# A split-precision decoder trunk on one core: where the first weight sum of a seven-product 2x2 block multiplication is made, and in which order its blocks are rounded

## The chip, the cores and the metric

One core of a Trainium2 chip runs the whole program. The metric is the device time of one execution in microseconds (us), the median over several runs; smaller is better.

## The reference, cut to what matters

Two layers, each FFN, mixer, FFN, on 256 tokens of width 1024. The four FFNs (F0, F1, F2, F3) are all alike:

```python
def swiglu(x, w_in, w_out):
    gate, up = jnp.split(x @ w_in, 2, axis=-1)      # w_in 1024 x 5632
    return (jax.nn.silu(gate) * up) @ w_out         # w_out 2816 x 1024
# x <- LN(ALPHA * x + 0.5 * swiglu(x, w_in, w_out))
```

The order of stages is F0, AB (attention and pooling), F1, F2, C (a gated recurrence), F3. The change touches the FFNs only.

## The kernel before, in words

**Split precision.** Every weight block lands in `raw` as float32. ScalarE (ACT) rounds it to a high part `w_hi` (`split_hi`, L503), VectorE (DVE) makes the rest `w_lo = raw - w_hi` (`split_lo`, L995), and TensorE (PE) adds three passes: high times high, high times rest, rest times high.

**Units.** A unit is 128 x 2048 numbers (1 MB), loaded as two transfers on SyncE's queue (SP) into one of three landing buffers. `raw_free` (L375) lets a load start when the last reader of that buffer is done. An FFN has eleven chunks of 256 hidden features. Each chunk needs two input units (called A and B here) and one output unit. Chunks 0 and 1 come in the plain form. Chunks 2 to 9 are feature-major: PE computes the hidden features transposed, in four up blocks (`up_block`, 16 matmuls each, L2012 and L2019), and ACT copies each block out of the one PSUM bank that they share (`up_copy`, L573), so up block b+1 waits for copy b. POOL folds the halves of the gate copies by accumulating transfers (`add_gates`, L1717), ACT takes the silu, DVE adds the halves of the up part and multiplies (`up_add`, `up_product`).

**Seven products.** For chunks 0 to 8 the output projection of a chunk, a 2x2 block product, is made of seven block products instead of eight (Winograd's form). Its weight unit, called P here, holds four plain blocks b12, b11, b22, b21, and four sums of them are needed. DVE makes the sums from `raw` into `SUM_PLACES` (`weight_sums`): t1 = b11-b12 and t3 = b22-b12 in one instruction (L1013), t2 = b22+t1 (L1017), t4 = b21-t2 (L1019). Three plain blocks are rounded into slot PLAIN (`split_plain_hi` L509, `split_plain_lo` L1001, 1536 columns), four sums into slot SUMS (`split_sums_hi` L515, `split_sums_lo` L1031, 2048 columns). Products 0, 1, 2 read PLAIN, products 3, 4, 5, 6 read SUMS.

**Order in chunk c.** Each engine runs a list written out by hand; nothing is reordered.
- PE (`feature_chunk`): up block 0; products 3 and 6 of P(c-2); up block 1; products 0, 1, 2 of P(c-1) begin; up block 2; their rest, which frees PLAIN (`plain_used`); product 4 begins; up block 3; products 4 and 5.
- ACT: the four copies, with the splits of A and B of chunk c+1 and of the sums between them, then the PLAIN split of P(c) before copy 3, then copy 3 and the gates' silu. In the last chunk (9), where there is no further P, the unit after B, called O here (the plain output unit of chunk 9), is split before copy 3; O takes slot PLAIN and so waits for `plain_used` too.
- DVE: add, product and hidden sums of chunk c-1 (`hidden_sums`); `weight_sums` of P(c-1); rests of the hidden sums; the rests of A, of the sums, of B and of P(c). Before chunk 2 it makes the rests of two units (chunk 2's A and B), hidden sums and the rest of P(1).
- POOL: `add_gates` for each chunk in turn.
- SP: P, A, B, P, A, B and so on, each when its buffer is free. P(c) uses the buffer of P(c-1), which is free when both the sums and the plain rest of P(c-1) are made.

After chunk 9 PE runs `project` for chunk 10, which waits for the last copy, and `down`, which waits for `last_hidT` (L1271) on DVE. The sums of the products leave PSUM by `kept` (L655), L664, `sums_out` and four accumulating transfers on POOL (`add_sums`, L1720).

Of the kernel before, what the change touches and what calls it, by code (L numbers as in the profile page):

```python
# [17 lines left out]
ALU = mybir.AluOpType  # L18
ACT = mybir.ActivationFunctionType
# [18 lines left out]
FIRST_FM = 2  # L38
N_FM = NC - 1 - FIRST_FM
# [36 lines left out]
def build(nc, x, positions, ln_gain, ln_bias, ffn1_w_in, ffn1_w_out, ffn2_w_in, ffn2_w_out, ab_w_in, ab_w_o,  # L76
          diff_lambda, diff_subln, pool_w, pool_scale, c_w_in, c_w_o, c_norm, hgrn_gamma, consts, out):
    with ExitStack() as ctx:
# [67 lines left out]
        w_step1, w_step2, w_sums = sem("w_step1"), sem("w_step2"), sem("w_sums")  # L146
        sums_hi, sums_lo, sums_used = sem("sums_hi"), sem("sums_lo"), sem("sums_used")
        sums_half = sem("sums_half")
# [119 lines left out]
        def region(a, *shape):  # L268
# [8 lines left out]
            return v  # L277

# [199 lines left out]
        def _(act):  # L478
# [26 lines left out]
            def split_plain_hi(n):  # L505

                landed(n)
                freed(plain_free[nth[n] - 1])
                nc.scalar.copy(w_hi[:, PLAIN, 0:1536], raw[:, n % RAW, 512:]).then_inc(plain_hi, 1)  # L509

            def split_sums_hi(name, n):

                act.wait_ge(w_sums, nth[n])
                freed(sums_free[nth[n] - 1])
                nc.scalar.copy(w_hi[:, SUMS], SUM_PLACES[name].rearrange("p a f -> p (a f)")).then_inc(sums_hi, 1)  # L515
# [65 lines left out]
            def ffn(name, m):  # L581
# [3 lines left out]
                if m == 0:  # L585
# [3 lines left out]
                    split_plain_hi(s0 + 4)  # L589
# [10 lines left out]
                else:  # L600
# [7 lines left out]
                    split_plain_hi(s0 + 4)  # L608
                    xT_split(m, 1)
                    act.wait_ge(hid_ready, hid + 1)  # L610
                    ffn_silu(name, 0, 1, G[1])
                    split_sums_hi(name, s0 + 4)
# [9 lines left out]
                split_plain_hi(s0 + 7)  # L622
                last = NC - 2
                for c in range(FIRST_FM, NC - 1):
                    n = s0 + 3 * c + 1
                    if c == FIRST_FM:
                        up_copy(name, c, 0)
                        hid_early_hi(name, c - 1)
                        hid_late_hi(name, c - 1)
# [3 lines left out]
                        up_copy(name, c, 2)  # L633
                        split_hi(n + 2)
                    elif c == FIRST_FM + 1:
                        up_copy(name, c, 0)
                        split_hi(n + 1)
                        hid_early_hi(name, c - 1)
                        hid_late_hi(name, c - 1)
                        up_copy(name, c, 1)  # L640
                        split_sums_hi(name, n)
                        split_hi(n + 2)
                        up_copy(name, c, 2)
                    else:
                        split_hi(n + 1)
                        up_copy(name, c, 0)
                        hid_early_hi(name, c - 1)
                        hid_late_hi(name, c - 1)
# [1866 lines left out]
```

## Time and profile before

| what | value |
|---|---|
| median of 3 runs | 966.76 us (966.62 to 968.57) |
| the profiled execution | 964.49 us, span 962.8 us |
| busy PE, PEld, DVE, ACT, POOL | 952.3, 806.8, 849.0, 620.4, 108.7 us |
| granted TensorE clock, mean | 0.998 |
| DMA, mean | 205 GB/s |

PE is TensorE's matmuls and PEld its weight loads, which run beside them. Busy time is time with at least one instruction on the engine. A line such as L573 is the line of the kernel that issued the instruction, and `[2.56 <-PE psum L2019]` behind a row of the timeline is how long the engine sat idle before it and what ended that.

### The profile page before, as it was taken

The numbers are of one execution on the slowest core, as the hardware profiler recorded it, in microseconds if no ns is written. First come the engines' busy times: TensorE is split into PE (matmuls) and PEld (weight loads), VectorE is DVE, ScalarE is ACT, GpSimd is POOL, SyncE is SP. The second block draws the span as 40 slices with busy tenths as digits, with TensorE's granted clock in tenths as the row PEclk, the third lists the DMA queues.
The fourth block names the chain that finished last, engine by engine and source line by source line (L and its number), as shares of the span: only waits on it lengthen the run. The fifth ranks groups of instructions, "written<-read, shape, count | busy, mean of one in ns | idle before, by whom it ended". The sixth has DMA issues, their size and how long they took to land.

```text
span 962.8 us, 13790 instructions
## 1 busy us (share of the span) xinstructions
PE 952.3 (99%) x4904; PEld 806.8 (84%) x4904; DVE 849.0 (88%) x1174; ACT 620.4 (64%) x727; POOL 108.7 (11%) x146
## 2 busy tenths in 40 slices
PE   9999999999999999999999999999999999999996
PEld 7888888888888888888888888888888888888885
DVE  5999998996898999889889989899898997999886
ACT  6776667436646667675576666549998546667660
POOL 0211111100210111110011101100100100111110
PEclk9999999999999999999999999999999999999999
DMA  9778877753656786876587777935243656786761
GB/s 306 240 228 234 280 235 223 232 178 129 223 180 205 217 244 193 236 227 206 173 237 235 239 231 232 271 124 184 89 131 115 235 192 190 215 242 194 237 162 55
DMA packets 140912, 197.31 MB, mean 205 GB/s; under 512 B 7280, under 2 KB 114336, under 8 KB 140720
## 3 DMA queue, kind: packets, MB, share of 16 engines
q1 hardware_dynamic: 126032, 173.56, 55.3%
q0 software_dynamic: 14256, 22.38, 11.1%
q8 instruction: 40, 0.66, 0.3%
q10 hardware_dynamic: 560, 0.52, 0.2%
q14 instruction: 24, 0.20, 0.1%
HBM read 182.79 MB, written 1.06 MB: 191 GB/s over the span
## 4 chain that ended last, share of the span: by engine, by line
PE 91%; DVE 5%; ACT 2%; issue 1%; DMA 1%; POOL 0%; DVEq 0%; SPq 0%; ACTq 0%
PE psum L2012 23%; PE psum L2026 15%; PE psum L2019 12%; PE psum L1821 12%; PE psum L1830 12%; PE psum L1825 12%; DVE w_lo L995 1%; PE psum L2402 1%; ACT w_hi L503 1%; PE psum L1814 1%; PE psum L2388 1%; DVE w_lo L1031 1%; DMA raw<-in_ffn_w_out 1%; DVE w_lo L1001 1%; PE psum L1996 1%
## 5 line engine op out<-in xcount | busy, mean ns | idle before, releaser
L995 DVE TENSOR_TENSOR w_lo<-raw,w_hi 128x2048 fp32r<-128x2048 f32 x125 | 285.1, 2284 | 20.9 <-ACT w_hi L503 20.8
L2012 PE MATMUL psum<-xT,w_hi 128*128 128x512 f32 x1024 | 254.2, 390 | 0.5
L503 ACT CAST w_hi<-raw 128x2048 fp32r<-128x2048 f32 x125 | 238.3, 1914 | 24.5 <-DMA raw<-in_ffn_w_in 15.0
L2012 PEld LDWEIGHTS psum<-xT,w_hi 128*128 128x128 f32 x1024 | 191.3, 188 | 44.8 <-ACT ffn_tok L573 3.2
L2019 PEld LDWEIGHTS psum<-xT,w_lo 128*128 128x128 f32 x1024 | 139.7, 190 | 10.0
L2019 PE MATMUL psum<-xT,w_lo 128*128 128x256 f32 x1024 | 142.8, 282 | 0.0
L1821 PE MATMUL psum<-w_hi,xT 128*128 128x512 f32 x447 | 128.7, 399 | 0.8 <-DVE arena L1538 0.4
L1830 PE MATMUL psum<-w_hi,xT 128*128 128x512 f32 x447 | 124.8, 390 | 0.2 <-DVE xT L1099 0.2
L1825 PE MATMUL psum<-w_lo,xT 128*128 128x512 f32 x447 | 124.7, 390 | 0.0
L1717 POOL DMA_DIRECT2D ffn_tok<-ffn_tok x64 | 55.0, 859 | 484.7 <-ACT ffn_tok L573 484.7
L1830 PEld LDWEIGHTS psum<-w_hi,xT 128*128 128x128 f32 x447 | 83.9, 188 | 18.3 <-DVE xT L1099 0.5
L1825 PEld LDWEIGHTS psum<-w_lo,xT 128*128 128x128 f32 x447 | 83.9, 188 | 17.7
L1821 PEld LDWEIGHTS psum<-w_hi,xT 128*128 128x128 f32 x447 | 80.8, 188 | 16.8 <-DVE ffn_tok L1160 0.8
L573 ACT COPY arena<-psum 128x512 f32<-128x512 f32 x64 | 37.6, 587 | 71.2 <-PE psum L2019 71.1
L1031 DVE TENSOR_TENSOR w_lo<-arena,w_hi 128x2048 fp32r<-128x2048 f32 x35 | 80.0, 2284 | 0.1
L1001 DVE TENSOR_TENSOR w_lo<-raw,w_hi 128x1536 fp32r<-128x1536 f32 x36 | 63.1, 1754 | 15.9 <-ACT w_hi L509 15.9
L573 ACT COPY ffn_tok<-psum 128x512 f32<-128x512 f32 x64 | 37.5, 586 | 59.3 <-PE psum L2019 45.1
L515 ACT CAST w_hi<-arena 128x2048 fp32r<-128x2048 f32 x36 | 68.9, 1915 | 10.5 <-DVE arena L1019 8.9
L2026 PE MATMUL psum<-w_hi,hT_hi 128*128 128x512 f32 x232 | 75.4, 395 | 0.0
L2026 PE MATMUL psum<-w_lo,hT_hi 128*128 128x512 f32 x232 | 75.1, 393 | 0.0
L2026 PE MATMUL psum<-w_hi,hT_lo 128*128 128x512 f32 x232 | 69.8, 393 | 0.0
L509 ACT CAST w_hi<-raw 128x1536 fp32r<-128x1536 f32 x36 | 53.5, 1485 | 14.5 <-PE psum L2026 7.9
(220 smaller groups left out, 1165.3 us busy)
## 6 DMA issues: line engine op xcount, KB each, us to landing
raw<-in_ffn_w_in SPq DMA_DIRECT2D x170, 512.0 KB, 5.2
raw<-in_ffn_w_out SPq DMA_DIRECT2D x88, 512.0 KB, 4.4
raw<-in_c_w_in SPq DMA_DIRECT2D x32, 512.0 KB, 4.7
ffn_tok<-ffn_tok POOLq DMA_DIRECT2D x64, 128.0 KB, 4.9
raw<-in_ab_w_in SPq DMA_DIRECT2D x16, 512.0 KB, 4.9
x_tok<-arena POOLq DMA_DIRECT2D x16, 256.0 KB, 7.3
raw<-in_ab_w_o SPq DMA_DIRECT2D x8, 512.0 KB, 4.2
raw<-in_c_w_o SPq DMA_DIRECT2D x8, 512.0 KB, 4.0
```

Of the source, the lines that this page charges most:

```text
L503: nc.scalar.copy(w_hi[:, slot_of[n]], raw[:, n % RAW]).then_inc(hi_ready, 1)
L515: nc.scalar.copy(w_hi[:, SUMS], SUM_PLACES[name].rearrange("p a f -> p (a f)")).then_inc(sums_hi, 1)
L573: nc.scalar.copy((UPS[name] if b // 2 else GATES)[:, b % 2], G[0]).then_inc(up_copied, 1)
L995: nc.vector.tensor_tensor(w_lo[:, slot_of[n]], raw[:, n % RAW], w_hi[:, slot_of[n]].bitcast(F32), ALU.subtract).then_inc(lo_ready, 1)
L1001: nc.vector.tensor_tensor(w_lo[:, PLAIN, 0:1536], raw[:, n % RAW, 512:], w_hi[:, PLAIN, 0:1536].bitcast(F32), ALU.subtract).then_inc(plain ...
L1031: nc.vector.tensor_tensor(w_lo[:, SUMS], SUM_PLACES[name].rearrange("p a f -> p (a f)"), w_hi[:, SUMS].bitcast(F32), ALU.subtract).then_in ...
L1821: nc.tensor.matmul(dst, a_hi, b_hi, start=first, stop=False)
L1825: ins = nc.tensor.matmul(dst, a_hi, b_lo, start=False, stop=final and last)
L1830: ins = nc.tensor.matmul(dst, a_lo, b_hi, start=False, stop=final and last)
L2012: nc.tensor.matmul(G[0], w_hi[:, slot_of[n + kh], at:at + P], xT_both[:, 4 * kh + k].rearrange("p a s -> p (a s)"), start=kh == k == 0, st ...
L2019: ins = nc.tensor.matmul(G[0][:, 0:SEQ], w_lo[:, slot_of[n + kh], at:at + P], xT_hi[:, 4 * kh + k], start=False, stop=kh == 1 and k == 3)
L2026: return nc.tensor.matmul(PROD[p], a[:, A_OF[p] * P:(A_OF[p] + 1) * P], w[:, slot, part * 512:(part + 1) * 512], start=start, stop=stop)
```

## The change

The unit P is loaded in the same way, but its first sum is made in place, in the landing buffer: the first quarter of `raw` becomes s1 = b12+b11. For P(0) and P(1) DVE does it (`first_sum`, 128 x 512), for P(2) to P(8) POOL does it with two accumulating transfers of 128 x 256 each, issued behind the gate transfers of the same chunk. The whole unit is now rounded into PLAIN (2048 columns), and only three sums go into SUMS (1536 columns): n2 = b22-s1 and, in one instruction, n2+b11 and n2+b21. Some signs turn, and with them those of the sums taken out at the end of an FFN. Product 4 becomes a plain product. So PE sets `plain_used` only behind up block 3, and POOL, ACT and DVE wait for each other in a new order: ACT's PLAIN split of P(c) stands behind the silu and waits for the first sum, DVE's PLAIN rest stands in the next chunk, in front of the rests of A, of the sums and of B, and ACT splits A between copy 1 and copy 2 in all chunks.

```diff
+HERE = 2
+        def first_sum_ready(name, n):
+            f, c = SILUS[name], (n - phases[name] - 4) // 3
+            if c < HERE:
+                return first_sum_here, HERE * f + c + 1
+            return first_sum_added, 32 * ((N_PROD - HERE) * f + c - HERE + 1)
...
 ACT
-            def split_plain_hi(n):
+            def split_plain_hi(name, n):
                 landed(n)
+                act.wait_ge(*first_sum_ready(name, n))
                 freed(plain_free[nth[n] - 1])
-                nc.scalar.copy(w_hi[:, PLAIN, 0:1536], raw[:, n % RAW, 512:]).then_inc(plain_hi, 1)
+                nc.scalar.copy(w_hi[:, PLAIN], raw[:, n % RAW]).then_inc(plain_hi, 1)
...
                 for c in range(FIRST_FM, NC - 1):
+                    up_copy(name, c, 0)
+                    hid_early_hi(name, c - 1)
+                    hid_late_hi(name, c - 1)
                     if c == FIRST_FM:
                         up_copy(name, c, 1)
                         split_hi(n + 1)
                         split_sums_hi(name, n)
...
                     else:
                         split_sums_hi(name, n)
                         up_copy(name, c, 1)
+                        split_hi(n + 1)
+                    up_copy(name, c, 2)
+                    split_hi(n + 2)
                     if c == last:
-                        act.wait_ge(plain_used, N_PROD * (f + 1))
-                        nc.scalar.activation(kept[0], PROD[0], ACT.Copy, scale=NORMS[name][1]).then_inc(copied_out, 1)
                         split_hi(n + 3)
-                    else:
-                        split_plain_hi(n + 3)
                     up_copy(name, c, 3)
                     gates_silu(name, c)
+                    if c < last:
+                        split_plain_hi(name, n + 3)
+                act.wait_ge(plain_used, N_PROD * (f + 1))
+                nc.scalar.activation(kept[0], PROD[0], ACT.Copy, scale=NORMS[name][1]).then_inc(copied_out, 1)
...
 DVE
+            def first_sum(n):
+                w = raw[:, n % RAW]
+                dve.wait_ge(raw_landed[n % RAW], 32 * (n // RAW))
+                nc.vector.tensor_tensor(w[:, 0:512], w[:, 0:512], w[:, 512:D], ALU.add).then_inc(first_sum_here, 1)
...
                 split_lo(s0 + 6)
+                first_sum(s0 + 7)
                 hidden_sums(name, 1)
                 split_plain_lo(s0 + 7)
...
-                    weight_sums(name, n, 0)
-                    weight_sums(name, n, 1)
...
+                    weight_sums(name, n)
...
+                    else:
+                        split_plain_lo(n)
+                        hid_early_lo(name, c - 1)
+                        hid_late_lo(name, c - 1)
+                        beside(name, c)
+                        split_sums_lo(name, n)
+                        split_lo(n + 1)
                     split_lo(n + 2)
-                    if c < last:
-                        split_plain_lo(n + 3)
...
 POOL
+            def first_sum(name, c):
+                n = phases[name] + 4 + 3 * c
+                w = raw[:, n % RAW]
+                pool.wait_ge(raw_landed[n % RAW], 32 * (n // RAW))
+                for cs in (slice(0, 256), slice(256, 512)):
+                    pool.dma_start(w[:, cs], w[:, 512 + cs.start:512 + cs.stop], accum_op=ALU.add
+                                   ).then_inc(first_sum_added, 16)
...
+                    if HERE <= c < N_PROD:
+                        first_sum(name, c)
...
 PE, feature_chunk
-                token_rest(last, 0, 1, 2).then_inc(plain_used, 1)
-                pe.wait_ge(sums_hi, nth[p])
+                token_rest(last, 0, 1, 2)
                 high(4)
                 up_block(name, n, c, 3)
+                weight_rest(4)
+                token_rest(last, 4).then_inc(plain_used, 1)
+                pe.wait_ge(sums_hi, nth[p])
                 high(5)
                 pe.wait_ge(sums_lo, nth[p])
-                weight_rest(4, 5)
-                token_rest(last, 4, 5).then_inc(pairs_done if last else early_used, 1)
+                weight_rest(5)
+                token_rest(last, 5).then_inc(pairs_done if last else early_used, 1)
```

At the start of an FFN the first sum of P(0) is made by DVE ahead of `weight_sums`, ACT rounds P(0) behind one more silu (in F1, F2 and F3), and product 4 joins product 0. At its end the one addition to x of 128 x 1024 (L1237) becomes an addition and a subtraction of 128 x 512.

## Rows read from the trace of the kernel before

**Rows 1.** The page, part 1: busy time of each engine.
```profile
PE 952.3 (99%) x4904; PEld 806.8 (84%) x4904; DVE 849.0 (88%) x1174; ACT 620.4 (64%) x727; POOL 108.7 (11%) x146
```

**Rows 2.** Who waited for whom: engine, line, waited for, us, times, longest.
```profile
PEld psum L2012 <- ACT ffn_tok L573: 3.2, 7, 0.6
```

**Rows 3.** The chain in order of time, F1: start, us, what.
```profile
350.18 1.81 PE psum L2012 x8
...
366.11 1.81 PE psum L2012 x8
```

**Rows 4.** Groups of instructions: busy us, mean ns, idle before.
```profile
L1031 DVE TENSOR_TENSOR w_lo<-arena,w_hi 128x2048 fp32r<-128x2048 f32 x35 | 80.0, 2284 | 0.1
...
L515 ACT CAST w_hi<-arena 128x2048 fp32r<-128x2048 f32 x36 | 68.9, 1915 | 10.5 <-DVE arena L1019 8.9
...
L1001 DVE TENSOR_TENSOR w_lo<-raw,w_hi 128x1536 fp32r<-128x1536 f32 x36 | 63.1, 1754 | 15.9 <-ACT w_hi L509 15.9
...
L1013 DVE TENSOR_TENSOR arena<-raw 128x1024 f32<-128x1024 f32 x36 | 43.8, 1218 | 3.1 <-DMA raw<-in_ffn_w_out 2.8 <-issue 0.2
...
L1017 DVE TENSOR_TENSOR arena<-raw,arena 128x512 f32<-128x512 f32 x36 | 24.9, 691 | 1.2
```

**Rows 5.** Timeline of F1 up to chunk 2's second up block.
```profile
288.70 1.22 DVE L1419 CAST decay<-arena 128x2048 fp32r<-128x2048 f32 x1
...
294.68 4.48 DVE L995 TENSOR_TENSOR w_lo<-raw,w_hi 128x2048 fp32r<-128x2048 f32 x2
...
296.48 1.49 ACT L509 CAST w_hi<-raw 128x1536 fp32r<-128x1536 f32 x1
...
300.53 0.59 ACT L573 COPY ffn_tok<-psum 128x512 f32<-128x512 f32 x1 [2.56 <-PE psum L2019]
...
301.49 0.64 PEld L2012 LDWEIGHTS psum<-xT,w_hi 128*128 128x128 f32 x3
```

**Rows 6.** Timeline of one undisturbed chunk of F1.
```profile
350.88 0.90 SPq L422 DMA_DIRECT2D raw<-in_ffn_w_out  x2
...
353.79 6.22 SPq L393 DMA_DIRECT2D raw<-in_ffn_w_in  x4
353.86 0.86 POOL L1717 DMA_DIRECT2D ffn_tok<-ffn_tok  x1 [3.31 <-ACT ffn_tok L573]
...
361.45 0.69 DVE L1067 TENSOR_TENSOR arena<-arena 128x512 f32<-128x512 f32 x1 [0.29 <-ACT arena L573]
```

**Rows 7.** DMA issues, 349.5 to 350.5 us: KB each, median us to landing.
```profile
ffn_tok<-ffn_tok POOLq DMA_DIRECT2D x1, 128.0 KB, 2.7
```

**Rows 8.** DMA issues, 350.8 to 352 us.
```profile
raw<-in_ffn_w_out SPq DMA_DIRECT2D x2, 512.0 KB, 4.3
```

**Rows 9.** DMA issues, 353.5 to 355 us.
```profile
ffn_tok<-ffn_tok POOLq DMA_DIRECT2D x1, 128.0 KB, 5.1
```

**Rows 10.** DMA issues of the whole program.
```profile
x_tok<-arena POOLq DMA_DIRECT2D x16, 256.0 KB, 7.3
```

**Rows 11.** Timeline of the end of F1.
```profile
421.57 0.60 ACT L655 ACTIVATE arena<-psum 128x512 f32<-128x512 f32 x1 [0.34 <-PE psum L2026]
...
423.99 2.29 DVE L995 TENSOR_TENSOR w_lo<-raw,w_hi 128x2048 fp32r<-128x2048 f32 x1 [1.63 <-ACT w_hi L503]
...
424.56 0.59 ACT L573 COPY arena<-psum 128x512 f32<-128x512 f32 x1 [0.60 <-PE psum L2019]
424.60 0.62 PE L2026 MATMUL psum<-w_lo,hT_hi 128*128 128x512 f32 x2
...
426.89 1.07 PE L1821 MATMUL psum<-w_hi,xT 128*128 128x512 f32 x4
...
437.30 0.42 DVE L1271 TENSOR_TENSOR hT_lo<-psum,hT_hi 128x256 fp32r<-128x256 f32 x1 [0.60 <-ACT hT_hi L676]
...
438.95 0.62 PE L1830 MATMUL psum<-w_hi,hT_lo 128*128 128x512 f32 x2
...
444.17 0.42 DVE L1160 TENSOR_TENSOR ffn_tok<-psum,ffn_tok 128x256 f32<-128x256 f32 x1 [0.21 <-ACT ffn_tok L540]
```

More of the change, by code:

```diff
@@ L514, in split_sums_hi @@
                 freed(sums_free[nth[n] - 1])
-                nc.scalar.copy(w_hi[:, SUMS], SUM_PLACES[name].rearrange("p a f -> p (a f)")).then_inc(sums_hi, 1)
+                nc.scalar.copy(w_hi[:, SUMS, 0:1536], SUM_PLACES[name][:, 1:].rearrange("p a f -> p (a f)")
+                               ).then_inc(sums_hi, 1)
             def split_hi_piece(n, k):
@@ new lines, in split_plain_lo, with weight_sums @@
+                nc.vector.tensor_tensor(w_lo[:, PLAIN], raw[:, n % RAW], w_hi[:, PLAIN].bitcast(F32), ALU.subtract
+                                        ).then_inc(plain_lo, 1)
+            def first_sum(n):
+                w = raw[:, n % RAW]
+                dve.wait_ge(raw_landed[n % RAW], 32 * (n // RAW))
+                nc.vector.tensor_tensor(w[:, 0:512], w[:, 0:512], w[:, 512:D], ALU.add).then_inc(first_sum_here, 1)
+            def weight_sums(name, n):
+                w = raw[:, n % RAW].rearrange("p (a f) -> p a f", a=4)
+                s1, b22, n2 = w[:, 0], w[:, 2], SUM_PLACES[name][:, 1]
+                dve.wait_ge(*first_sum_ready(name, n))
+                if nth[n] > 1:
+                    dve.wait_ge(sums_lo, nth[n] - 1)
+                nc.vector.tensor_tensor(n2, b22, s1, ALU.subtract).then_inc(w_step, 1)
+                dve.wait_ge(w_step, nth[n])
+                nc.vector.tensor_tensor(SUM_PLACES[name][:, 2:4], w[:, 1:4:2], n2.unsqueeze(1).to_broadcast([P, 2, 512]),
+                                        ALU.add).then_inc(w_sums, 1)
@@ L1031, in split_sums_lo @@
-                nc.vector.tensor_tensor(w_lo[:, SUMS], SUM_PLACES[name].rearrange("p a f -> p (a f)"),
-                                        w_hi[:, SUMS].bitcast(F32), ALU.subtract).then_inc(sums_lo, 1)
+                sums = SUM_PLACES[name][:, 1:].rearrange("p a f -> p (a f)")
+                parts = ((0, 512, sums_first), (512, 1536, sums_lo)) if halves else ((0, 1536, sums_lo),)
+                for c0, c1, signal in parts:
+                    nc.vector.tensor_tensor(w_lo[:, SUMS, c0:c1], sums[:, c0:c1], w_hi[:, SUMS, c0:c1].bitcast(F32),
+                                            ALU.subtract).then_inc(signal, 1)
@@ L1963, in _ @@
             A_OF = (2, 3, 6, 0, 4, 5, 1)
-            B_OF = ((PLAIN, 0), (PLAIN, 2), (PLAIN, 1), (SUMS, 3), (SUMS, 0), (SUMS, 1), (SUMS, 2))
+            B_OF = ((PLAIN, 1), (PLAIN, 3), (PLAIN, 2), (SUMS, 2), (PLAIN, 0), (SUMS, 0), (SUMS, 1))
             ALONE = (0, 4, 5, 6)
@@ L1981, in products @@
                 if half:
[L1982 removed]
+                    pe.wait_ge(sums_first, 1)
                 else:
```

89 lines of the change are left out of this document (22 added, 67 removed).

## The prediction, on record before the changed kernel ran

> **What bounds the kernel now.** I read the page's busy times first. TensorE is busy 952.3 of a span of 962.8 us, VectorE 849.0 [rows 1]: PE is the bound nearly everywhere, and its matmuls number the same before and after this change. So a lighter DVE can give back only what PE now waits. The list of waits gives that directly. The one wait of PE inside the feature-major chunks that repeats is that of an up block for ACT's copy of the one before it: 3.2 us in 7 places [rows 2]. It comes up in the first chunks of each FFN, where DVE's queue is the late one. In an undisturbed chunk the chain in order of time repeats its second up block from 350.18 to 366.11, that is every 15.93 us, with PE on the chain throughout [rows 3]. The ceiling of the gain is therefore 3.2 us, and every new wait is measured against it.
>
> **The change part by part.**
>
> *DVE's work.* Today a P unit costs DVE 1.22 + 0.69 + 0.69 for the sums, 1.75 for the plain rest, 2.28 for the sums' rest [rows 4], the third instruction taken as long as the second, of the same shape. After it, 0.69 + 1.22 for the sums, 2.28 plain and 1.75 sums, and 0.69 more for P(0) and P(1) only. That is 0.69 less for 28 of 36 units, 19 us of DVE in all. PE hides all of it but the 3.2 us. I take the whole **-3.2 us**: in chunks 2 and 3 DVE loses both 0.69 and the plain rest of 1.75 from in front of `up_add`.
>
> *ACT's work.* The two casts swap sizes and their sum stays.
>
> *Start of the chunks, P(1).* Today ACT rounds P(1) at 296.48, long before it has to copy up block 0 at 300.53; it sat idle 2.56 us before that copy [rows 5]. After the change this cast waits for the first sum, which DVE makes only behind two rests that run from 294.68 for 4.48 us, to 299.16 [rows 5]. First sum to 299.88, cast of 1.92 [rows 4] to 301.8, copy of 0.59 to 302.3. PE's second up block loads its first weights at 301.49 today [rows 5], without a wait, and would start at 302.35: **+0.85 us**, in each of four FFNs, 3.4. Who waits behind the cast on ACT: copy 0, the hidden parts, copy 1. In F1 there is more. DVE used the time before 288.70 for a sums' rest, then made the table cast of 1.22 us [rows 5]; now it must wait for a hidden product first and makes the sums' rest behind it, so that the table cast pushes the hidden sums out by 1.4 us; PE then waits some 0.75 us more by my count. F0 has the plain split behind the landing and the first sum, 0.3 us more net. Together **+4.45 us**; bounds 2.4 (only half of 0.85 is paid, plus extras of half size) and 6.
>
> *Waits for the first sum in the loop.* Count from the undisturbed chunk. `up_add` started at 361.45, so one chunk earlier at 345.5 [rows 3, 6]. In the new order B's rest ends just before it, and I take 345.8. Add, product and hidden sums take 2.5 us with their semaphores, the new sums 0.69 + 1.22, the plain rest 2.28 [rows 4]: 352.5, when the landing buffer of P is free. SP issues the next P at 352.7 where it now does at 350.88 [rows 6], its second transfer 0.45 later, landing after 4.3 [rows 8]: 357.45. POOL wakes and issues the first accumulating transfer, and the second behind it, which I put at 0.95 together (an estimate; one issue alone is busy 0.86 [rows 6]): the second starts at 358.4. What does a transfer of 128 KB by POOL take? The gate transfer alone on the queues took 2.7 us [rows 7], the one issued at 353.86 beside the loads of A issued at 353.79 [rows 6] took 5.1 [rows 9]. In the new order A's buffer is free behind the early and late rests (1.24), the sums' rest 1.75 and A's own rest 2.28, at 357.7, so A is loaded just when the first sum is made. I take 5.1, since the row has the same company: the first sum is there at 363.5. ACT needs 1.92 + 0.59 from there to have up block 0 copied: 366.05, and PE starts the second up block at 366.11 [rows 3]. So it just fits, or is a few tenths late, since there are two such transfers. A wait is paid at every second chunk: one paid at a chunk moves PE, but not the chain behind the next P, by its length. That makes 14 payments in four FFNs. Taken: 0.2 us each, **+2.6 us**. Bounds: 0, and (with the 7.3 us of the accumulating transfers into x [rows 10]) 2.2 x 14 = 31 us.
>
> The row shows a gate transfer nearly doubled by company [rows 7, 9]. The Trainium skill, page "DMA: Bandwidth & Descriptors", section "Queues, rings and completion order", says that an engine takes turns between queue rows only at packet boundaries; the trace agrees, with 2.7 against 5.1 us. The same page, section "Anatomy of one DMA — SWDGE (gpsimd) path", fits one such transfer by 2.0 us plus its bytes over 436 KB per us, an estimate of 2.3 us here; by it there would be no wait at all and the sum would be 2.6 us less.
>
> *End of an FFN.* Here I expect the largest term. In chunk 9 ACT splits O, into slot PLAIN, ahead of copy 3. PLAIN was freed before up block 3, at 421.5 (L655 at 421.57 waited for it) [rows 11]. Now it is freed behind up block 3 and two matmuls, as the row at 424.60 shows, near 425.0. The cast runs 425.0 to 426.9, copy 3 to 427.45 instead of 425.15. PE's `project`, at 426.89 today [rows 11], waits for copy 3: **+0.6 us**. DVE is worse off: O's rest moves from 423.99 [rows 11] to 426.95, and `up_add` stands behind it, so the whole DVE list, with the hidden part, the sums out and three more rests, is 3.0 us late. By my count over the timeline it has 0.9 us of idle time on its way to `last_hidT`, 0.60 of it right in front [rows 11]. I count it through to 440.0 instead of 437.30, ending 440.4, while PE reaches the first pass that reads it at 438.95 + 0.6 [rows 11]: 0.85 more. The hidden product of the second tile, at 444.17 [rows 11], comes behind a norm on DVE and costs 0.75 more. Sum 2.2 us per FFN with a following stage, and 0.6 in F3, where DVE has no units of a next stage to split: **+7.2 us**. Bounds: 0.6 x 4 = 2.4, and 3.0 x 4 = 12. The addition to x in two parts costs 0.16 us more of DVE and lies inside this.
>
> *The rest.* POOL issues 56 more transfers; it is busy 108.7 us [rows 1], so nobody queues there. kept[0] is copied later, and PE needs it only a projection later.
>
> **Sum.** 4.45 + 2.6 + 7.2 - 3.2 = +11.05 us on the profiled execution's 964.49: 975.5. The median of the runs lies 2.3 above that execution, so I forecast **977.8 us**.
>
> **The rivals.**
> 1. *The first sum lands as if alone* (2.7 us [rows 7]): no waits in the loop, 964.49 + 8.45 + 2.3 = 975.2. For it: A is issued only as the sum starts. Against: so it was for the gates. The fit of the Trainium skill's page "DMA: Bandwidth & Descriptors" is the rule that points here.
> 2. *The end is absorbed*: DVE's lateness of 3.0 us is made up in the last projection, and only 0.6 x 4 remains, with no loop waits: +3.65, 970.4. For it: many waits on DVE there are for ACT. Against: DVE idles only 0.9 us before `last_hidT`.
> 3. *The first sum takes longer*: 6.2 us, halfway from 5.1 to 7.3 [rows 9, 10], two accumulating transfers and two loads at once. Then 1.1 us x 14 = 15.4 instead of 2.6, and 990.6 us. For it: three queued accumulating transfers take 7.3. Against: those have twice the bytes.
> 4. *Costs and gain cancel*: the two start and end costs are each paid at their lower bound and the gain is whole: 2.4 + 2.4 - 3.2 = +1.6, 968.4 or a little less.
> 5. *DVE's relief decides*: ACT's two late casts (P(1) and O) are covered by waits that PE has anyway, and 3.2 us of PE's waits go: 963.6. It would decide if copy 0 of chunk 2 still ended by 301.5 and copy 3 of chunk 9 by 426.9. Against: the orders of ACT and DVE are fixed, and both dates follow from rows alone.
> 6. *It doesn't do what it says*: if the accumulating transfers gave no relief because DVE still waits at `up_add` for copy 3 (0.29 us idle there today [rows 6]), DVE's 19 us turn into idle time. That holds in the undisturbed chunks in any case, and is in the sum.
>
> **How the numbers follow.** A measurement here tells apart about 0.2%, 1.9 us. Chances: forecast 0.40, rival 1 0.13, rival 2 0.15, rival 3 0.16, rival 4 0.08, rival 5 0.08. Slower is then 0.84, within 0.2% 0.08, faster 0.08. The range reaches from a little below rival 2 to just short of rival 3's time, 968.5 to 990.0. The forecast's own range is 973 to 983.
>
> **What would show it.** In the profile of the changed kernel: ACT's plain cast of P(1) begins near DVE's first sum, and the second up block of chunk 2 waits 0.8 us for copy 0. Undisturbed chunks still take 15.9 us, and DVE is busy 0.7 us less in each. The list of waits has ACT's plain cast waiting for the accumulating transfer in many chunks. At FFN ends ACT's split of O waits for PE some 1.5 us and more, `project` waits for copy 3, and a `down` pass for L1271. I am wrong if the waits of PE for ACT in the chunks fall below 3.2 us in total, or if an FFN from its chunk 2 to its last `down` is not 3 us or more longer than before.

## The result, and the profile after

The changed kernel takes **1024.47 us** (median of 5 runs, 1017.31 to 1026.87) against 966.76 (965.39 to 970.18) on the same chip: ratio 1.057, 95% interval 1.054 to 1.060. It is 57.7 us slower, where 11 were forecast. Its profiled run has a span of 1023.7 us, 60.9 more than before.

The page of the changed kernel, busy times and the software queue:
```profile
PE 970.7 (95%) x4904; PEld 813.2 (79%) x4904; DVE 833.8 (81%) x1150; ACT 612.4 (60%) x727; POOL 157.5 (15%) x202
...
q0 software_dynamic: 22320, 29.72, 15.7%
```
DVE is 15.2 us lighter than in [rows 1], near the forecast 19, and it bought nothing. PE is busy 18 us *more* with the same 4904 matmuls: some of them ran at a lower clock.

The changed kernel's groups (busy us, mean ns, idle before) that answer to [rows 4]:
```profile
L998 DVE TENSOR_TENSOR w_lo<-raw,w_hi 128x2048 fp32r<-128x2048 f32 x36 | 82.4, 2290 | 6.9 <-ACT w_hi L519 6.3
...
L525 ACT CAST w_hi<-arena 128x1536 fp32r<-128x1536 f32 x36 | 53.3, 1481 | 0.0
...
L1016 DVE TENSOR_TENSOR arena<-raw,arena 128x1024 f32<-128x1024 f32 x36 | 44.1, 1225 | 1.2
```
The compute prices were right. The waits of the changed kernel (engine, line, waited for, us, times, longest), against [rows 2]:
```profile
POOL raw L1716 <- DMA raw<-in_ffn_w_out: 84.4, 28, 4.8
ACT w_hi L519 <- issue: 68.5, 23, 4.5
...
PEld psum L2020 <- ACT ffn_tok L584: 42.4, 25, 3.3
...
DVE arena L1014 <- DMA raw<-raw: 19.8, 18, 2.2
...
PEld psum L1829 <- ACT hT_hi L673: 8.3, 2, 4.3
...
PEld psum L1829 <- ACT arena L584: 3.6, 4, 0.9
```
Read from PE backwards. L2020 is the up block: its waits for copy 0 were 3.2 us in 7 places and are 42.4 in 25. Copy 0 stands behind ACT's plain cast L519, and that cast waits 68.5 us for something the profile shows only as "issue"; DVE's L1014, which waits for the same first sum, names it: the transfer raw<-raw. It lands late in nearly every chunk:
```profile
raw<-raw POOLq DMA_DIRECT2D x56, 128.0 KB, 5.5
```
From each FFN's first up block of chunk 2 to its last of chunk 9, the four FFNs take 136.10, 133.70, 135.82 and 135.42 us instead of 124.24, 124.04, 124.45 and 124.32: **44.0 of the 60.9 us** are there, the waits at the chunks' start among them. The other 16.9 lie from there to the next FFN: 6.5 (F0 to F1), 7.4 (F1 to F2), 2.0 (F2 to F3), 0.9 (after F3) and 0.1 ahead of F0.

In F1, PEld's waits at the second up blocks of chunks 2 to 9 are 0.88, 3.26, none, 1.73, 0.20, 1.63, none, 1.78: the start, and then every second chunk, as forecast, but some eight times its size each. The other three FFNs don't keep to that: F2 has 2.42, 1.65 and 2.05 in chunks 3, 4 and 5, F3 waits in every chunk from 5 to 9, F0 in 3, 5, 6, 8 and 9. In all, 21 of the 28 chunks behind a sum by POOL wait, 38.9 us together. The largest wait has a tail. Timeline of the changed kernel, chunk 3 of F1:
```profile
337.41 1.90 ACT L519 CAST w_hi<-raw 128x2048 fp32r<-128x2048 f32 x1 [4.55 <-issue]
...
339.22 0.58 ACT L584 COPY ffn_tok<-psum 128x512 f32<-128x512 f32 x1
...
339.85 3.06 PEld L2020 LDWEIGHTS psum<-xT,w_hi 128*128 128x128 f32 x8 [3.26 <-ACT ffn_tok L584]
339.85 3.57 PE L2020 MATMUL psum<-xT,w_hi 128*128 128x512 f32 x8 [2.83 <-ACT ffn_tok L584]
...
345.36 1.98 PE L2020 MATMUL psum<-xT,w_hi 128*128 128x512 f32 x8
```
and the windows of the same stretch (us, engines, granted clock, DMA share, GB/s):
```profile
339.84:343.40 3.56, 3.55 (x10) 2.86 (x11) 3.56 (x4) 2.26 (x3) 0.85 (x1) 0.55 0.41 77
343.40:347.00 3.60, 3.60 (x22) 3.11 (x21) 1.14 (x2) 2.40 (x2) 0.85 (x1) 1.00 0.82 266
374.77:378.30 3.53, 3.53 (x19) 3.09 (x20) 3.53 (x4) 2.69 (x4) 0.86 (x1) 1.00 0.38 62
```
After PE had stood still for 2.83 us the eight matmuls took 3.57 us instead of 1.98, at a granted clock of 0.55, mostly the lower level of 1.2 GHz, and the next up block came 5.51 us later instead of 3.93: 1.6 us on top of the wait. After the wait of 1.3 us (PE) at 374.77 the clock stayed at 1.00. The same loss of 1.6 to 1.7 us follows five of the 21 waits (PE idle for 1.8 to 2.8 us), 8.3 us in all. The length of the wait alone doesn't decide it: after 1.99 us at 535.59 the clock stayed at 1.00. The Trainium skill, page "TensorE: Matmul & The Clock Gate", section "What's actually happening", has a gate that passes half or all of the pulses by how busy PE was of late; the trace agrees, with 0.55 against 1.00.

### The profile page after: what moved, and what is told of

It reads as the page before. It is cut to its first block, busy times and chain, and to the rows that moved or that the text cites. A ratio compares the mean times of both kernels' runs of the same rounds, so it can differ in the third digit from the quotient of the medians.

```text
span 1023.7 us, 13823 instructions
## 1 busy us (share of the span) xinstructions
PE 970.7 (95%) x4904; PEld 813.2 (79%) x4904; DVE 833.8 (81%) x1150; ACT 612.4 (60%) x727; POOL 157.5 (15%) x202
## 4 chain that ended last, share of the span: by engine, by line
PE 62%; DVE 12%; DMA 10%; issue 8%; ACT 6%; SPq 1%; POOL 1%; DVEq 0%; ACTq 0%
PE psum L2020 16%; PE psum L2034 9%; PE psum L1829 8%; PE psum L1833 8%; PE psum L1838 8%; PE psum L2027 8%; DMA raw<-in_ffn_w_out 4%; DVE w_lo L992 4%; DMA raw<-in_ffn_w_in 2%; DMA raw<-raw 2%; ACT w_hi L512 2%; DVE w_lo L998 2%; ACT w_hi L519 1%; ACT ffn_tok L584 1%; DMA raw<-in_ab_w_in 1%
## 5 line engine op out<-in xcount | busy, mean ns | idle before, releaser
L992 DVE TENSOR_TENSOR w_lo<-raw,w_hi 128x2048 fp32r<-128x2048 f32 x125 | 285.6, 2288 | 90.4 <-ACT w_hi L512 90.2
L2020 PE MATMUL psum<-xT,w_hi 128*128 128x512 f32 x1024 | 262.8, 400 | 32.0 <-ACT ffn_tok L584 31.8
L512 ACT CAST w_hi<-raw 128x2048 fp32r<-128x2048 f32 x125 | 238.5, 1916 | 39.0 <-DMA raw<-in_ffn_w_in 11.1
L2020 PEld LDWEIGHTS psum<-xT,w_hi 128*128 128x128 f32 x1024 | 194.4, 192 | 83.4 <-ACT ffn_tok L584 42.4
L2027 PEld LDWEIGHTS psum<-xT,w_lo 128*128 128x128 f32 x1024 | 141.1, 192 | 10.5
L519 ACT CAST w_hi<-raw 128x2048 fp32r<-128x2048 f32 x36 | 68.7, 1907 | 83.1 <-issue 68.5
L998 DVE TENSOR_TENSOR w_lo<-raw,w_hi 128x2048 fp32r<-128x2048 f32 x36 | 82.4, 2290 | 6.9 <-ACT w_hi L519 6.3
L2034 PE MATMUL psum<-w_lo,hT_hi 128*128 128x512 f32 x232 | 80.4, 394 | 0.0
L2034 PE MATMUL psum<-w_hi,hT_lo 128*128 128x512 f32 x232 | 75.1, 393 | 0.0
L1025 DVE TENSOR_TENSOR w_lo<-arena,w_hi 128x1536 fp32r<-128x1536 f32 (+2 forms) x37 | 63.1, 1708 | 0.1
L1716 POOL DMA_DIRECT2D raw<-raw x56 | 48.7, 1023 | 84.4 <-DMA raw<-in_ffn_w_out 84.4
```

The source lines that it names most:

```text
L512: nc.scalar.copy(w_hi[:, slot_of[n]], raw[:, n % RAW]).then_inc(hi_ready, 1)
L519: nc.scalar.copy(w_hi[:, PLAIN], raw[:, n % RAW]).then_inc(plain_hi, 1)
L992: nc.vector.tensor_tensor(w_lo[:, slot_of[n]], raw[:, n % RAW], w_hi[:, slot_of[n]].bitcast(F32), ALU.subtract).then_inc(lo_ready, 1)
L998: nc.vector.tensor_tensor(w_lo[:, PLAIN], raw[:, n % RAW], w_hi[:, PLAIN].bitcast(F32), ALU.subtract).then_inc(plain_lo, 1)
L1025: nc.vector.tensor_tensor(w_lo[:, SUMS, c0:c1], sums[:, c0:c1], w_hi[:, SUMS, c0:c1].bitcast(F32), ALU.subtract).then_inc(signal, 1)
L2020: nc.tensor.matmul(G[0], w_hi[:, slot_of[n + kh], at:at + P], xT_both[:, 4 * kh + k].rearrange("p a s -> p (a s)"), start=kh == k == 0, st ...
```

## The experiments

Each is an edit of the changed kernel. The first question was whether the late landing is the cause, and of how much; the rivals were the new order of the rests on DVE, the order at an FFN's end, and the clock. The kernel before took 966 to 967 us (median) on each occasion. "Product 4 early" and the like name edits of chunk 9, the last feature-major one.

**First sums by DVE.** `first_sum` of P(2) to P(8) goes to DVE, ahead of B's rest.
```diff
-HERE = 2
+HERE = 9
                         split_lo(n + 1)
+                    if c < last and c < HERE:
+                        first_sum(n + 3)
                     split_lo(n + 2)
```


> The changed kernel, but DVE makes all first sums (one add of 128x512 in front of B's rest, where DVE stood idle 1.6 us waiting for ACT); orders of ACT and PE as changed. Theory T (the landing of the transferred first sum, late on the cycle load - sum - casts - load, makes the chunks of an FFN 9.7 to 11.9 us longer each, 44 us in four): the 32 chunks return to 15.9 to 16.2 us and the time falls by 40 to 46 us, to 979 to 985. Rival O (the new order of the rests on DVE and the later release of PLAIN make the chunks long, whoever makes the sum): over 1010 us, chunks stay over 16.8 us.


Measured: **977.47 us** (976.33 to 978.79), ratio 1.012 (1.010 to 1.014). 47.0 us are gone, a little more than the 40 to 46 expected. The chunks are back at 15.93 us but for one or two in each FFN (to 16.8). Waits of this kernel:
```profile
PEld psum L1831 <- ACT arena L584: 3.6, 4, 0.9
...
PEld psum L2022 <- ACT ffn_tok L584: 3.4, 4, 0.9
...
PEld psum L1831 <- ACT hT_hi L673: 2.9, 3, 2.3
```
So moving the first sums from POOL to DVE gives 47 us back, and the order of the rests on DVE, which is the changed one here too, is not the cause. Not all of it is the loop: of the 49.1 us between the two profiled spans (1023.7 and 974.6), 42.3 lie between an FFN's first up block of chunk 2 and its last of chunk 9, and 6.8 between the FFNs. What stays is 0.9 us at each start, 0.9 at each `project`, and a wait for the hidden part.

**The end, first try.** O split behind copy 3 and the silu, its rest behind `up_product`.
```diff
-                    if c == last:
-                        split_hi(n + 3)
                     up_copy(name, c, 3)
                     gates_silu(name, c)
                     if c < last:
                         split_plain_hi(name, n + 3)
+                    else:
+                        split_hi(n + 3)
...
-                split_lo(n + 3)
                 up_add(name, last)
                 up_product(name, last)
+                split_lo(n + 3)
```


> The changed kernel, but in the last chunk ACT splits O only behind copy 3 and the silu, and DVE makes O's rest behind up_product. Theory E (O's split, waiting for PLAIN, holds copy 3, up_add and with them the whole end of an FFN, and the units loaded next): PE's waits of 4.3 and 3.6 us for the hidden part's copy at two FFN ends go, 9 to 14 us less than the changed kernel, 1011 to 1016. Rival (the end is late because O's rest is late in any order, as PLAIN is freed late): less than 4 us gained, since O's rest comes 2 us later still here.


Measured: 1025.92 us (1024.0 to 1033.68), ratio 1.061. No gain. In its profile (of the slowest execution) PE's waits for copy 3, 3.6 us in the changed kernel, are gone, but those for the hT_hi copy (ACT's rounding of the last chunk's hidden part, L673, which `down` reads) are 12.3 us in 3 places instead of 8.3 in 2: O's rest comes later still, and the load behind it too. This run does not separate the two. That DVE's queue, my reason for the end term, is not what PE waits for is seen in the changed kernel: there no matmul waits for L1268 (`last_hidT`, L1271 before), and PEld waits for L1154 (L1160 before) 1.3 us in 2 places.

**One transfer instead of two.**
```diff
-            return first_sum_added, 32 * ((N_PROD - HERE) * f + c - HERE + 1)
+            return first_sum_added, 16 * ((N_PROD - HERE) * f + c - HERE + 1)
...
-                for cs in (slice(0, 256), slice(256, 512)):
-                    pool.dma_start(w[:, cs], w[:, 512 + cs.start:512 + cs.stop], accum_op=ALU.add
-                                   ).then_inc(first_sum_added, 16)
+                pool.dma_start(w[:, 0:512], w[:, 512:D], accum_op=ALU.add).then_inc(first_sum_added, 16)
```


> The changed kernel with one accumulating transfer of 128x512 instead of two of 128x256. Theory T with issue as a part of the lateness: the second issue started 0.87 us behind the first, so the sum is there 0.3 to 0.9 us sooner, and at 14 to 28 payments the time falls by 5 to 20 us. Rival B (the bytes beside the loads set the landing, not the number of issues): within 4 us of the changed kernel.


Measured: 1007.89 us (1002.18 to 1013.27), ratio 1.044 (1.038 to 1.049), 16.6 us less. One transfer of 256 KB takes 6.0 us, hardly more than one of 128 KB (5.5), and the second issue, 0.87 us on POOL, is saved:
```profile
raw<-raw POOLq DMA_DIRECT2D x28, 256.0 KB, 6.0
```

**Loads kept apart.** SP holds A's loads until the first sum is there.
```diff
-                    with sp.Fori(0, NPAIR) as i:
...
+                    for c in range(2 * NPAIR):
+                        a = s0 + 5 + 3 * c
+                        if c >= HERE:
+                            sp.wait_ge(first_sum_added, 32 * ((N_PROD - HERE) * SILUS[name] + c - HERE + 1))
+                        for kh in range(2):
+                            load_gate_up(a + kh, None, wi, kh, c + 2)
+                        load_rows(a + 2, None, wo, c + 1)
```


> The changed kernel, but SP issues A's loads only once the first sum of the P before it has landed, so the two do not run side by side (the loads of chunks 2 to 9 are written out instead of looped). Theory C (company: a transfer of POOL takes 2.7 us alone and 5.5 beside loads): the first sum lands in about 3.5 us, 2 us sooner, most waits go, 20 to 40 us less, 985 to 1005. Rival (its length is its own, or A's later landing at once takes its place as the wait): less than 8 us gained, or a loss.


Measured: 1021.29 us (1018.63 to 1026.2), ratio 1.059, far from the 985 to 1005 that theory C expected. The DMA issues of this kernel:
```profile
raw<-in_ffn_w_out SPq DMA_DIRECT2D x88, 512.0 KB, 6.0
...
ffn_tok<-ffn_tok POOLq DMA_DIRECT2D x64, 128.0 KB, 6.5
...
raw<-raw POOLq DMA_DIRECT2D x56, 128.0 KB, 3.1
```
Without the company of the loads the transfer takes 3.1 us instead of 5.5. The company isn't gone but moved: the gate transfers take 6.5 (3.6 in the changed kernel), the loads of output units, P's among them, 6.0 (4.4), and POOL's wait for P's landing is 155.0 us instead of 84.4. So this run shows that company lengthens the transfer, and not what a shorter one would be worth.

**Every second sum by POOL.** My theory by then was that lateness is carried from P to P, since load, sum and rests take as long as a chunk.
```diff
-HERE = 2
+HERE = (0, 1, 3, 5, 7)
...
-                    if HERE <= c < N_PROD:
+                    if c < N_PROD and c not in HERE:
                         first_sum(name, c)
...
+                    if c in HERE:
+                        first_sum(n + 3)
```


> DVE makes the first sum of P(3), P(5), P(7), POOL that of P(2), P(4), P(6), P(8), as in the changed kernel. All POOL sums replaced by DVE sums took 47.0 us off (1024.5 to 977.5), over 28 chunks, 1.68 us each. Theory L (lateness is carried from one P to the next, since the round trip of load, sum and plain rest is as long as a chunk): a chunk of DVE between two of POOL gives the next P its early issue back, so a POOL chunk then pays only what a single one is short of, some 0.7 us (first sum there at 352.7 + 5.1 + 0.9 + 5.5 = 364.2 against 363.5), 16 of them: 977.5 + 11 = 989, chunks behind a DVE sum at 15.9 to 16.1 us. Rival N (each POOL sum pays by itself, nothing is carried): 16 x 1.68 = 27, 1004.


Measured: **1017.06 us** (1012.23 to 1024.79), ratio 1.053 (1.049 to 1.057). Both expectations fail: 16 sums by POOL cost 39.6 us over the 977.47, 2.5 each, nearly as much as all 28 together. So nothing needs to be carried: all 16 wait, and none of the chunks between them. Each sum that meets an undisturbed PE pays in full; one behind a paid wait meets a PE that is late already and pays less. That is the prediction's "every second chunk", but it is only partly so: in the changed kernel the sums behind a paid wait pay nothing in F1 (or 0.2 us) and in part elsewhere. By PEld's waits for copy 0 without the four starts, 16 sums cost 34.9 us here and 28 cost 38.9 there. Timeline of this kernel, one clean cycle, P(8) of F1:
```profile
424.12 1.98 PE L2024 MATMUL psum<-xT,w_hi 128*128 128x512 f32 x8
...
426.59 0.90 SPq L433 DMA_DIRECT2D raw<-in_ffn_w_out  x2
...
431.84 5.00 SPq L404 DMA_DIRECT2D raw<-in_ffn_w_in  x4
...
432.23 1.74 POOL L1720 DMA_DIRECT2D raw<-raw  x2 [3.40 <-DMA raw<-in_ffn_w_out]
...
439.25 0.69 DVE L1016 TENSOR_TENSOR arena<-raw 128x512 f32<-128x512 f32 x1 [1.03 <-DMA raw<-raw]
439.30 1.90 ACT L521 CAST w_hi<-raw 128x2048 fp32r<-128x2048 f32 x1 [3.24 <-issue]
...
441.10 0.58 ACT L586 COPY ffn_tok<-psum 128x512 f32<-128x512 f32 x1
...
441.73 1.66 PE L2024 MATMUL psum<-xT,w_hi 128*128 128x512 f32 x6 [1.52 <-ACT ffn_tok L586]
```
Undisturbed, the up block at 441.73 would have started at 424.12 + 15.93 = 440.05. This is the cycle that the prediction forecast, ending at the kernel before's
```profile
365.95 1.98 PE L2012 MATMUL psum<-xT,w_hi 128*128 128x512 f32 x8
```
The prediction compared with 366.11, where the chain of [rows 3] has this block, while its other dates come from the timeline, which has it at 365.95. The two cycles side by side, in us before the block's undisturbed start in the timeline:

| | forecast | measured |
|---|---|---|
| P's load issued | 13.25 | 13.46 |
| P landed, first accumulating issue | 8.50 | 7.82 |
| second one starts | 7.55 | 6.95 |
| first sum is there | 2.45 | 0.80 |
| up block can start | -0.10 | -1.68 |

Against the forecast "just fits", 0.60 us are lost by the landing and the issue, 1.05 by the transfer (6.15 instead of 5.1), and 0.16 by the two dates of one block. P(2) is dearer: in the changed kernel's F1 its load is issued 1.4 us later against PE (324.63, where the up block began at 320.79), so its wait is 3.3 us (2.4 to 3.1 in the other FFNs), and there the low clock follows; it does so in three of the four FFNs.

**The start.** With DVE's sums, the first sum of P(1) ahead of the rest of B, in F1 to F3.
```diff
+                if m:
+                    first_sum(s0 + 7)
                 split_lo(s0 + 6)
-                first_sum(s0 + 7)
+                if m == 0:
+                    first_sum(s0 + 7)
```


> All first sums on DVE in the loop (977.5 us), and in F1, F2 and F3 the first sum of P(1) stands in front of the rest of chunk 2's B instead of behind it. Theory S (copy 0 of chunk 2 is late because ACT's cast of P(1) waits for that sum): the waits of the up block for copy 0, 0.9 us in each FFN, go in three FFNs: 974.8, between 974.5 and 975.5. Rival (the hidden sums, 0.7 us later on DVE for the same reason, or the cast itself is late by PE): 977.5, no change.


Measured: 977.13 us (974.04 to 980.44). No change in the median. The waits at the start went as expected (3.4 us in 4 places became 0.9 in one), but those for the hT_hi copy at FFN ends grew from 2.9 to 6.9 us.

**Product 4 early.** With DVE's sums; in chunk 9 alone PE ends product 4 before up block 3.
```diff
                 high(4)
-                up_block(name, n, c, 3)
+                if c < NC - 2:
+                    up_block(name, n, c, 3)
                 weight_rest(4)
                 token_rest(last, 4).then_inc(plain_used, 1)
+                if c == NC - 2:
+                    up_block(name, n, c, 3)
```


> All first sums on DVE in the loop (977.5 us), and in the last feature-major chunk alone PE does the rests of product 4 in front of up block 3, so that slot PLAIN is free there as early as in the kernel before. Theory E (the end of an FFN costs since O is split late, and with O's rest everything behind it on DVE and the loads of the next stage): the waits for copy 3 (3.6 us in 4 places) and for the first hT_hi copy of the next stage (2.9 us in 3) go: 971.0, between 969 and 973. Rival (as when O's split was put behind copy 3, the lateness comes from elsewhere, from the loads): 977.5, at best 976.


Measured: 982.01 us (981.21 to 983.35), ratio 1.017 (1.015 to 1.018), 4.5 us *more*, where theory E expected 971 and its rival no change. The waits for copy 3 are gone as expected, but those for the hT_hi copy are 10.9 us instead of 2.9. (That copy is of the last chunk of the same FFN, not of the next stage, as the expectation has it.)

**These two together.**


> The first sums on DVE in the loop, the first sum of P(1) early in F1, F2 and F3, and product 4 in front of up block 3 in the last feature-major chunk. If the two terms add: 977.5 - 2.7 - 6.5 = 968.3, within 0.2% of the kernel before (966.4). If DVE's relief of 0.69 us per chunk is not there any more (DVE makes the first sum again) and the second DVE wait stays, 970 to 972. The rival (neither does anything): 977.5.


Measured: 979.71 us (977.91 to 984.75). That is neither the sum of the two (968.3) nor a gain at all. The terms don't add while something else at the end can eat them.

What eats them is seen in the changed kernel's timeline at the end of F1:
```profile
448.76 0.59 ACT L584 COPY arena<-psum 128x512 f32<-128x512 f32 x1 [1.53 <-PE psum L2027]
...
449.24 1.91 ACT L512 CAST w_hi<-raw 128x2048 fp32r<-128x2048 f32 x1
...
449.72 1.98 PE L2020 MATMUL psum<-xT,w_hi 128*128 128x512 f32 x8
...
453.50 13.98 SPq L402 DMA_DIRECT2D raw<-in_ffn_w_in  x8
...
455.15 2.29 DVE L992 TENSOR_TENSOR w_lo<-raw,w_hi 128x2048 fp32r<-128x2048 f32 x1 [1.67 <-ACT w_hi L512]
...
457.40 2.62 POOL L1728 DMA_DIRECT2D x_tok<-arena  x3 [10.83 <-ACT arena L661]
...
468.73 1.90 ACT L512 CAST w_hi<-raw 128x2048 fp32r<-128x2048 f32 x1 [5.30 <-DMA raw<-in_ffn_w_in]
...
470.53 0.37 ACT L673 CAST hT_hi<-psum 128x256 fp32r<-128x256 f32 x1
470.95 0.50 PEld L1829 LDWEIGHTS psum<-w_hi,hT_hi 128*128 128x128 f32 x2 [4.29 <-ACT hT_hi L673]
```
O's buffer is given back by O's rest at 457.44 us; the load into it, for the next FFN, is issued at 457.47 and 457.88, beside three accumulating transfers into x from 457.40 on. The second half lands 10.8 us after its issue. ACT splits that unit at 468.73, in front of the hT_hi copy, and PE waits 4.29 us for the copy. In the kernel before, the same load was issued at 426.31 and 426.72, O's rest having begun at 423.99 [rows 11], with the transfers into x from 426.62 on; its second half took 6.4 us, and nobody waited. The PE wait at 470.95 is followed by the low clock too (0.50 from there to 476.20). O is late not only through `plain_used`: in the changed order ACT splits B *behind* copy 2 (the cast at 449.24), and O behind B.

**A and B early in chunk 9.** With DVE's sums, in that chunk alone.
```diff
 ACT
-                    else:
+                    elif c < last:
...
+                    else:
+                        split_hi(n + 1)
+                        split_sums_hi(name, n)
+                        up_copy(name, c, 1)
+                        split_hi(n + 2)
                     up_copy(name, c, 2)
-                    split_hi(n + 2)
+                    if c < last:
+                        split_hi(n + 2)
...
 DVE
+                    elif c == last:
+                        split_plain_lo(n)
+                        hid_early_lo(name, c - 1)
+                        split_lo(n + 1)
+                        hid_late_lo(name, c - 1)
+                        beside(name, c)
+                        split_sums_lo(name, n)
```


> First sums on DVE in the loop (977.5 us). In the last feature-major chunk alone ACT splits A in front of the sums and B in front of copy 2, and DVE makes A's rest in front of the sums' rest, as the kernel before does. Theory Q (in the changed order B's rest is late, so the loads that take its buffer and O's buffer, for the next stage, are issued 2.5 us later against PE and the second of them runs beside the three transfers into x and takes 12 us instead of 6.8; ACT, which splits that unit in front of the hidden part, then holds PE): that load is issued some 1.5 us earlier than without it, the waits for the hT_hi copy shrink or go, 973 to 976 us. Rival W (O's split behind up block 3 holds that load in any case, since O's buffer is the one): no change, 977.5. The copy 3 waits (3.6 us) stay under both.


Measured: 978.78 us (976.32 to 979.6). No gain: rival W holds, O is still split behind up block 3.

**The same, with product 4 early.**


> As the run before, and product 4 in front of up block 3 in that chunk, so that O is split early too. Alone that second edit made it worse (982.0 us). Theory Q: now both buffers are given back about 1 us after where the kernel before does, before the transfers into x start; the waits for the hT_hi copy (10.9 us) and for copy 3 (3.6 us) go, and 969 to 972 us result. Rival X (product 4 in front does harm by itself, since the transfers into x start earlier by it): 977 or more, and the load is again beside those transfers.


Measured: **970.65 us** (968.83 to 971.92), ratio 1.004 (1.003 to 1.006). Each edit alone gave +1.3 and +4.5; together they take 6.8 off. Timeline of this kernel, end of F1:
```profile
424.57 1.91 ACT L512 CAST w_hi<-raw 128x2048 fp32r<-128x2048 f32 x1 [1.08 <-PE psum L2049]
...
426.51 2.29 DVE L998 TENSOR_TENSOR w_lo<-raw,w_hi 128x2048 fp32r<-128x2048 f32 x1 [1.66 <-ACT w_hi L512]
...
429.67 2.62 POOL L1743 DMA_DIRECT2D x_tok<-arena  x3 [8.78 <-ACT arena L667]
...
435.07 1.90 ACT L512 CAST w_hi<-raw 128x2048 fp32r<-128x2048 f32 x1
...
439.09 0.37 ACT L679 CAST hT_hi<-psum 128x256 fp32r<-128x256 f32 x1 [2.12 <-PE psum L2019]
```
O's rest ends at 428.80, the load is issued at 428.83, 0.84 us ahead of the transfers into x, and lands in 5.0 us (median of its halves); ACT's third cast waits for nothing, and the hT_hi copy waits for PE, not PE for it.

**All three edits.**


> As the run before, and the first sum of P(1) early in F1, F2 and F3. If the start (2.0 us of PE waits seen gone in the chunks) and the end add: 967 to 970 us; what then is left against the kernel before is F0's start and 0.6 us of DVE's first sums in chunk 3. Rival: 975 or more, if the start's gain is eaten at the FFN ends, as it was when it stood alone (977.1).


Measured: **966.64 us** (965.61 to 968.67, 12 runs), ratio 1.000 (0.999 to 1.001). The start's edit, worth nothing alone, is now worth 4.0 (2.6 between the two profiled spans).

What the edits at the end share is seen in the second half of the load that takes O's buffer, by the ends of F0, F1 and F2 (us; waits below 0.3 left out):

| kernel | issued, against the first transfer into x | issue to landing | PEld's wait for the hT_hi copy |
|---|---|---|---|
| before | 0.1 behind | 6.8, 6.4, 6.0 | none |
| changed | 0.5 behind | 10.5, 10.8, 6.6 | 4.0, 4.3, none |
| DVE's sums | 0.5 behind | 8.8, 6.9, 6.7 | 2.3, 0.4, none |
| DVE's sums, start | 0.5 behind | 9.9, 10.0, 6.6 | 3.4, 3.5, none |
| DVE's sums, product 4 | 0.6 behind | 10.8, 11.8, 10.8 | 3.3, 4.3, 3.3 |
| DVE's sums, start, product 4 | 0.6 behind | 11.7, 10.8, 10.6 | 4.2, 3.3, 3.1 |
| DVE's sums, A and B | 0.5 behind | 8.7, 6.7, 6.5 | 2.2, none, none |
| DVE's sums, A and B, product 4 | 0.4 ahead | 8.2, 5.5, 5.8 | none |
| DVE's sums, all three | 0.4 ahead | 6.0, 7.9, 5.1 | none |

Where the landing takes 8.7 us or more, PE waits 2.2 us or more; where it takes 8.2 or less, 0.4 at most.

**The three edits under POOL's sums.**


> The changed kernel, with its sums on POOL, and the three other edits (B and A of the last feature-major chunk early, product 4 in front of up block 3 there, the first sum of P(1) early in F1 to F3). With the sums on DVE the same three edits took 10.9 us off (977.5 to 966.6). If the late landing in the loop is a term of its own, it stands alone here: 966.6 + 47.0 = 1013.6, between 1010 and 1018, every late chunk start as in the changed kernel, and nothing at the FFN ends. Rival (the terms hide one another, since a PE that is late in the last chunk gives the loads time): 1005 or less, or 1021 and more if the edits do nothing under POOL's sums.


Measured: 1011.39 us (1008.64 to 1013.78), ratio 1.047 (1.045 to 1.049). The landing in the loop stands alone with 1011.39 - 966.64 = 44.8 us, next to the 47.0 of the first experiment. Between the two profiled spans it is 42.6 us, all of it from an FFN's first up block of chunk 2 to its last of chunk 9. This run also bounds the clock: it fell in only two places of the loops, and the loops are still this long. Its longest wait in F1 was followed by no fall:
```profile
334.36 2.11 PE L2036 MATMUL psum<-xT,w_hi 128*128 128x512 f32 x8 [2.70 <-ACT ffn_tok L584]
...
334.36:337.90 3.54, 3.54 (x19) 3.11 (x20) 3.54 (x4) 2.70 (x4) 0.85 (x1) 1.00 0.46 57
```

## Why the prediction was wrong

By the chain of runs, the 57.8 us over the last kernel are **47.0** for the sums back on DVE (1024.47 to 977.47), **6.8** for the order in chunk 9 (to 970.65) and **4.0** for the start (to 966.64). The forecast had 2.6 for the loop, 7.2 for the end and 4.45 for the start, less 3.2. The first step is not all loop: by itself the loop is 44.8 us in medians and 42.6 in spans. The changed kernel's own executions lie from 1017.31 to 1026.87, so the first step is known, by my estimate, to some 3 us.

- **Waits for the first sum in the loop: the step that failed.** Its mechanism and its place were right: copy 0 waits behind the PLAIN cast, which waits for the first sum, and P's load was issued within 0.2 us of the forecast. The term was mis-sized: +2.6 us, where the runs show 42.6 to 44.8. I found a first sum that "just fits, or is a few tenths late" and took 0.2 us; a clean cycle is 1.7 late. "So it just fits" was a difference of two dates 13 us apart, each of its transfers priced by a single row: 4.3 for P's landing (POOL woke 5.64 after the first issue, not 4.75) and 5.1 for the accumulating transfer (6.15; the model was one gate transfer, here are two in a row), and the date to keep was read 0.16 us late. Then up blocks wait for it in 21 places, not 14 (the list's 25 less the four starts): "every second chunk" holds in F1 alone. P(2)'s wait is 2.4 to 3.3 us, since DVE is later in chunk 2, and the fall of the clock adds 1.6 to 1.7 us in five places. The upper bound, 2.2 x 14 = 31 us, was itself too low, and I left it out of the range.
- **Rival 3** (a transfer of 6.2 us) had the duration that was measured, and still forecast 15.4 us, since it kept the early landing and the 14 places and had no clock. **Rival 1** (2.7 us, and the 2.3 us estimated by the fit in the Trainium skill's page "DMA: Bandwidth & Descriptors", section "Anatomy of one DMA — SWDGE (gpsimd) path") is refuted beside loads: 5.5 us in the median. Kept apart it took 3.1, so the company is what lengthens it, though how the DMA engines share their time no trace here shows; the fit is near a transfer with little company, and the measurement decides here.
- **The start of the chunks: right in mechanism and place, near in size.** Copy 0 held the second up block by 0.84 to 0.93 us (0.85 forecast) in each FFN, and mending it in three FFNs gave 4.0 us in medians, 2.6 in profiled spans, where the waits mended add up to some 2.6. F1's table cast was not tested by itself.
- **The end: near in size by luck, mostly wrong in reason.** 6.8 us against 7.2, but the changed kernel has 16.9 us more between its FFNs. With DVE's sums 10.1 are left of it, and the edits in chunk 9 take 11.2 there and cost 3.4 in the loops; 6.8 (7.8 in spans) is what remains. `project` waited 0.9 us for copy 3 in each FFN (0.6 forecast). The rest was not DVE's lateness on its way to `last_hidT`, for which no matmul of the changed kernel waited, but the second half of a load for the next stage, issued 0.5 us behind the transfers into x, where the kernel before has 0.1, and landing late, with the low clock behind the wait. The forecast had not seen that B moves behind copy 2 either. Rival 2, in which the end is absorbed, is refuted.
- **DVE's relief, -3.2 us:** not seen. Where the loop was mended, DVE makes the first sum itself, so that kernel has no relief and can't show it; under POOL's sums, 44.8 us of lateness cover it.

**What stays open:** why that load took 10.5 and 10.8 us at two ends of the changed kernel and 6.6 at the third, and 6.7 to 8.8 in the kernel with DVE's sums, at the same distance of issues (0.5 us). That the order of these transfers is behind the results of the start and of product 4 alone is read from their traces and from the runs that put the load ahead; the transfers into x were not moved by themselves.

## What to carry to other kernels

When an accumulating transfer replaces 0.7 us of an engine's work, price the whole chain from the load that feeds it to the engine that waits, each transfer by the longest row that has company, take all dates from one view, and compare with the slack; here a fit to within a tenth, over a load and two accumulating transfers, was a wait of 1.7 us. A wait can cost more than itself, by the clock. And edits that gain nothing alone can be worth their full price together: find what absorbs them before dropping them.

## What the runs showed of the hardware

- Accumulating transfers of 128 KB by POOL took 2.7 us where the next loads were issued 1.2 us behind it [rows 6, 7], 3.1 (median) with the loads held back, 5.5 (median) beside loads and 6.15 in the clean cycle; one of 256 KB took 6.0 where two of 128 KB took some 7 from the first issue. Two issues in a row on POOL start 0.87 us apart.
- Holding loads away from a transfer moved the contention onto other ones (medians: gate transfers from 3.6 to 6.5 us, loads of output units from 4.4 to 6.0).
- A 512 KB load issued 0.5 us behind the first of three accumulating transfers of 256 KB took 6.5 to 10.8 us in the kernels of the table above, with no cause found for the spread.
- PE idle for 2.83 us was followed by 3.56 us at a granted clock of 0.55; idle for 1.3 us it kept 1.00. Between these it went either way: 1.82 us of idle time was followed by a fall, 1.99 us and, in the last run, 2.70 us by none.
